# Cache pages shared 9 to 7 between SyncE and GpSimd, and the first gate blocks read ten chunks at a time

## The reference

```
g = jax.nn.softmax(cv, axis=-1)
act = jax.nn.gelu(jnp.einsum('nhkd,nd->nhk', expert_u[experts], x))
y = jnp.einsum('nhk,nhkd->nd', (g * act), expert_v[experts])
```

## Time and profile before

| what | value |
|---|---|
| time, median of three runs | 2148.72 us |
| the profiled execution: own time | 2147.01 us |
| the profiled execution: span | 2145.1 us |
| TensorE busy | 1915.8 us, 89% |
| VectorE busy | 1436.1 us, 67% |
| mean granted TensorE clock | 0.904 |
| granted clock, 400 to 600 us and 600 to 800 us | 0.68 and 0.67 |
| granted clock, 1400 to 1600 us | 1.00 |

### The profile page before, as it was taken

How to read it: one execution, slowest core, us unless ns; L and a number is a source line. 1 busy time by engine, 2 the same in 40 slices (tenths; PEclk the granted TensorE clock), 3 DMA queues, 4 the chain that set the end, 5 groups by cost and what they waited for, 6 DMA issues and landing times.

```text
span 2145.1 us, 26500 instructions
## 1 busy us (share of the span) xinstructions
PE 1915.8 (89%) x9117; PEld 1500.0 (70%) x9117; DVE 1436.1 (67%) x3189; ACT 609.1 (28%) x1020; POOL 586.6 (27%) x454
## 2 busy tenths in 40 slices
PE   6988899666688988999886999999999999999994
PEld 3556674554467745667675788888888888888883
DVE  4025366243346755999986778888888777777777
ACT  1132122210011111114455333333333333333331
POOL 0000002344423123310000114454454444444440
PEclk9989999666675679999998999999999999999997
DMA  6611334354534456554438878999998888888872
GB/s 250 228 40 40 123 118 162 108 164 146 186 137 147 148 171 229 202 178 149 164 141 302 295 278 321 356 349 340 364 340 301 317 289 291 320 287 292 318 255 92
DMA packets 152645, 479.29 MB, mean 223 GB/s; under 512 B 14624, under 2 KB 75856, under 8 KB 130928
## 3 DMA queue, kind: packets, MB, share of 16 engines
q1 hardware_dynamic: 94704, 270.60, 34.8%
q0 software_dynamic: 57856, 207.65, 27.2%
HBM read 443.73 MB, written 33.94 MB: 223 GB/s over the span
## 4 chain that ended last, share of the span: by engine, by line
PE 73%; DVE 16%; another core or an unknown queue 4%; DMA 3%; issue 2%; ACT 2%; POOL 0%; SPq 0%; DVEq 0%; ACTq 0%
PE ps L1034 24%; PE ps L1024 19%; PE ps L634 6%; PE ps L970 3%; PE ps L935 3%; PE ps L986 3%; DVE lo L1650 2%; PE ps L1011 2%; PE ps L721 2%; PE ps L720 2%; PE ps L803 2%; PE ps L743 1%; PE ps L638 1%; DMA lo<-x 1%
## 5 line engine op out<-in xcount | busy, mean ns | idle before, releaser
L1478 POOL DMA_INDIRECT lo<-ur,lo x192 | 244.3, 1272 | 797.8 <-DVE lo L2011 323.5
L1478 POOL DMA_INDIRECT lo<-vr,lo x192 | 278.1, 1448 | 650.1 <-DVE lo L2079 306.7
L1024 PE MATMUL ps<-xh,uh 128*128 128x352 f32 x832 | 270.6, 325 | 0.0
L1024 PE MATMUL ps<-xh,ul 128*128 128x352 f32 x832 | 270.5, 325 | 0.0
L1024 PE MATMUL ps<-xl,uh 128*128 128x352 f32 x832 | 268.8, 323 | 0.0
L1129 ACT ACTIVATE hi<-ps 128x512 f32<-128x512 f32 (+10 forms) x259 | 154.3, 645 | 373.7 <-PE ps L970 111.9
L1034 PE MATMUL ps<-vh,hh 128*128 128x512 f32 (+1 forms) x768 | 240.9, 395 | 19.9 <-DVE vl L2047 19.9
L1034 PE MATMUL ps<-vl,hh 128*128 128x512 f32 (+1 forms) x768 | 241.1, 395 | 0.0
L1034 PE MATMUL ps<-vh,hl 128*128 128x512 f32 (+1 forms) x768 | 240.0, 394 | 0.0
L2071 DVE SCALAR_TENSOR_TENSOR lo<-lo 128x1024 f32<-128x1024 f32 x174 | 221.8, 1282 | 18.5 <-DMA lo<-vr,lo 9.7
L2047 DVE TENSOR_TENSOR vl<-hi,vh 128x1024 fp32r<-128x1024 f32 x128 | 156.9, 1226 | 48.8 <-ACT vh L1129 48.3
(11 more groups left out here) (385 smaller groups left out, 2928.5 us busy)
## 6 DMA issues: line engine op xcount, KB each, us to landing
hi<-ev SPq DMA_DIRECT2D x64, 1024.0 KB
hi<-wts SPq DMA_DIRECT2D x22, 2048.0 KB, 7.8
hi<-eu SPq DMA_DIRECT2D x38, 1024.0 KB, 10.0
lo<-eu SPq DMA_DIRECT2D x26, 1024.0 KB
gates<-hi SPq DMA_DIRECT2D x11, 2048.0 KB, 7.2
hi<-gates SPq DMA_DIRECT2D x32, 704.0 KB, 8.5
lo<-cache SPq DMA_DIRECT2D x48, 128.0 KB
hi<-cache SPq DMA_DIRECT2D x48, 128.0 KB
```

The lines of the kernel that those rows point to most:

```text
L1024: last = nc.tensor.matmul(ps[:, 6 + p, 0:GW[1]], a[p][:, k * 128:(k + 1) * 128], b[:, k, :], start=(k == 0 and b is xh and a is uh), stop= ...
L1478: nc.gpsimd.indirect_dma_start(ring[n % RING], None, table, bass.IndirectOffsetOnAxis(idxs[:, i, k:k + 1], 0)).then_inc(r_in[n % RING], 16)
```

## The change

There are two parts. `SP_PAGES` goes from 12 to 9, so SyncE loads nine of the 16 pages of a round and GpSimd gathers seven. And the first two quads of gates are read from DRAM in two steps: once ten chunks are stored, SyncE reads these ten for both quads (`load_first_gates`), before it stores the last chunk; VectorE copies the last chunk's part from `stage[0]` into `gt`. ScalarE's first `round_v` stands ahead of the copies of the last chunk, its first `round_hidden` ahead of the wait for the last store, and VectorE's first `low_v` ahead of everything of the first block.

```diff
-SP_PAGES = 12
+SP_PAGES = 9
@@ sync
+            def load_first_gates(quad):
+                sp.dma_start(gt[quad].rearrange("p c b t -> p c (b t)")[:, 0:NCH - 1, :],
+                             table[:, 0:NCH - 1, quad * 4:quad * 4 + 4, :].rearrange("e c b t -> e c (b t)")).then_inc(g_in[quad], 16)
...
+                if c == NCH - 1:
+                    sp.wait_ge(gs_in[0], 16 * (NCH // 2))
+                    sp.wait_ge(gs_in[1], 16 * (NCH // 2))
+                    for quad in range(2):
+                        load_first_gates(quad)
                 sp.wait_ge(s["ev_done"], CH // 4 * (c + 1))
                 sp.dma_start(gates[c * NK:(c + 1) * NK, :], stage[c % 2].rearrange("p e t -> p (e t)")).then_inc(gs_in[c % 2], 16)
             load_v(1, 1)
             sp.wait_ge(gs_in[0], 16 * ((NCH + 1) // 2))
-            sp.wait_ge(gs_in[1], 16 * (NCH // 2))
-            for q in range(2):
-                load_gates(q, q)
@@ scalar
                     for q in range((T[i] - S0) // 4, (T[i] - S0 + r) // 4):
+                        if q == (NCH - 1) * CH // 4:
+                            round_v((0, 0), 16, None)
                         gates_copy(q)
...
+            round_hidden(0, 1, None)
             act.wait_ge(gs_in[0], 16 * ((NCH + 1) // 2))
-            round_v((0, 0), 16, None)
-            round_hidden(0, 1, None)
@@ vector
             dve.wait_ge(s["gm_ps"], GW[1] // 4)
+            low_v((0, 0), 1)
+            fetched_gates(0)
+            dve.wait_ge(gs_in[1], 16 * (NCH // 2))
+            dve.wait_ge(s["ev_done"], GW[1] // 4)
+            for quad in range(2):
+                ins = v.tensor_copy(gt[quad][:, NCH - 1], stage[(NCH - 1) % 2][:, quad * 4:quad * 4 + 4, :])
+            step(ins)
             early_gated(0)
             low_hidden(0, 1)
-            low_v((0, 0), 1)
-            fetched_gates(0)
```

## The result

| | before | changed kernel |
|---|---|---|
| median of four runs | 2143.88 us (2138.95 to 2148.87) | 2165.95 us (2158.09 to 2173.91) |
| ratio | | 1.0103, 95% interval 1.0053 to 1.0153 |
| the profiled execution: own time, span | 2147.01, 2145.1 us | 2164.88, 2163.1 us |

The changed kernel is 1.0% slower: the first case, and the sum of the prediction (2164.2 us for the profiled execution) met. That is only half of the story. On the four chips where the experiments ran, the kernel before takes 2079 us instead of 2144, and there the change costs 0.2%, hardly more than nothing. Both halves follow. The chip that it ran on is not on record, so the runs do not say whether it was a fifth chip or one of the four at another time.

What follows compares the result with a forecast made beforehand. TensorE bounds the second half, so sample rounds and the first expert block's start count: 2147.0 + 26.2 (gathers) - 9.0 (gates) = 2164.2 us for the profiled execution, median 2166 us (+0.8%), range 2115 to 2175.

Steps and rivals of the forecast that it cites:

- the first case: Sample rounds: release of VectorE's maximum tied to the end of GpSimd's run; 2157 to 2175 us, chance 0.58.
- Three more gathers in each run: Sample rounds: GpSimd's run ends 3.75 us later, and VectorE's release with it; +26.2 us over rounds 0 to 6.
- the upper end: Sample rounds: distance behind the run's end grows by another 0.5 us for each of 7 rounds; +30 us.
- the pattern: Sample rounds 1 to 6: VectorE's maximum starts 2.2 to 2.7 us behind GpSimd's last gather.
- the reading beneath: Sample rounds: after SyncE's and GpSimd's DMAs issue side by side, engines' signals arrive late until GpSimd's unbroken run ends.
- Gates ten chunks at a time: First expert block: gate reads issued after chunk 9's store let TensorE start earlier; gain 9 us, 7 to 11.
- the release follows SyncE's loads: Sample rounds: three loads less bring the release 2.2 us earlier in 7 rounds, -15.5 us; 2124 us, chance 0.16.
- pages are free: Sample rounds: release not tied to GpSimd's run, only the gates count; 2140 us (2134 to 2143), chance 0.14.
- The late release that goes away: Sample rounds: nine loads stay under the point where signals are held back, saving 57 us; 2083 us, chance 0.12.
- SyncE's tenth load: Sample rounds: condition of the 2083 us rival, that the holding of signals begins only with this load; chance 0.12.
- eight loads: First row fetches: VectorE was already held by "remote" with this many loads issued, argued against the 2083 us rival.

Runs made afterwards that it cites:

- the first comparison: Kernel before against the changed kernel, the measurement of the result table: 2143.88 and 2165.95 us, ratio 1.0103.
- before_again: Kernel before, without any edit, profiled again on one of the chips of the experiments: 2075.62 us in one run.
- g12_quad: Against the kernel before: pages twelve and four, new gate reading with only the first quad's read ahead of the last store; 2065.94 us, ratio 0.9941.
- p9_only: Kernel before with only SP_PAGES changed from 12 to 9, gates read as before: 2087.26 us, ratio 1.0041.

## Why the prediction was right, and where it was not

*Three more gathers in each run: right in the first comparison.* The forecast was 22.5 us for rounds 1 to 6; from the maximum of round 0 (404.72, now 410.97) to that of round 6 (586.15, now 615.03) it was 181.4 and is 204.1 us: 22.6. Two deviations cancel in it: the distance behind the run grew from 2.2 to 2.8 us (the upper end had 0.5 for it), and round 6 was released 3.5 us sooner than the pattern. Round 0, taken at 3.75 us, was held 4.2 us (406.75 to 410.97). Here the reading beneath was luck: the 1.94 us that it stood behind GpSimd's run before was no late release. In `before_again`, without any late signal, the same row stands 1.93 us behind the run, as TensorE's matmul only ends then. That matmul itself ended 2.1 us later in the changed kernel's execution, which nobody forecast. So the rounds end 28.9 us later, not 26.2, and the 26.9 at the gates come close to the forecast only because other stages took 2 us less. The "remote" total is 105.2 us without round 0, forecast 104.

*Gates ten chunks at a time: right.* The steps, in us:

| step | forecast | measured |
|---|---|---|
| issue of the reads to the first product | 5.2 at most | 4.6 |
| first product to TensorE | 1.7 | 1.9 |
| block 0 to block 1 | 7.9 | 8.1 |
| the last store, from its issue | 9.5 | 8.8 |
| block 1 to block 4 | 14.2 | 14.9 |
| gain in all | 9 | 9.1 |

TensorE's first gap shrank further than forecast, to 4.7 us from 7, as the idle time is counted from the end of its last gate matmul, which moved too. The step priced by no row of the trace before, a store behind reads in the queue, was bounded by 0 and 2.7 and taken at 2.2. From 7.3 us before, the store's landing became 8.8 here, 1.5 more. In the four traces of the experiments with both reads ahead it was 9.4 to 10.6, up to 3.4 more, so the upper bound was too low. `g12_quad` shows that the delay is real.

*The rivals.* That the release follows SyncE's loads is refuted by the changed kernel's own trace: 15.1 us from their end to the release with nine loads, 9.8 with twelve. That pages are free is refuted with late signals and without: the rounds of `p9_only` are 7.5 us longer. The late release that goes away (2083 us, chance 0.12, tied to "SyncE's tenth load") did not happen by the change. In the experiments it is absent from the kernel before as well: 2079 us before, 2084 changed. The price of the late releases was near (57 forecast, 59.0 in the rounds) and the condition wrong; that the rival's 2083 us fits the changed kernel's 2083.87 is luck, as it had nothing for GpSimd's full queue. The "eight loads" that the prediction sets against this rival are what its window shows of a burst of twelve; when VectorE started at 336.21 us, not even eight had been issued, so the argument stands.

*What was wrong is the reading beneath.* "Once SyncE's and GpSimd's DMAs have been issued side by side, signals of engines are delivered late": in the experiments they are issued side by side, up to 24 and 13 to a round, and no signal is late in any of twelve traces. The overlap may be needed, but it is not enough. That the last signal is delivered 2.2 to 2.8 us behind the end of GpSimd's run is seen in thirteen rounds of the two first traces (the last of them by ScalarE's wait), before and after the run was lengthened. The change itself was the only edit that moved it, as the late signals never came back. What brings them about, a chip, a state of it or something else, is open.

So 2166 us was met because the trace came from where the result was measured, and the last digits are luck. The fourth run of the kernel before moved its median from 2148.72 to 2143.88 us, so that the medians differ by 22.1 us where 17.2 were forecast; the two profiled executions differ by 17.9. There the parts are +26.9 and -9.1; in the experiments the same two are about +8.5 and -10.6 of a median near 2079 (from the two kernels apart, each within 5 us), and together measured at +3.5 us (0 to 7). The sign of the gates' part is the same in both; the size of the pages' part is not.

## What to carry to other kernels

When a wait has no releaser in the trace, ask first whether the same kernel shows it on another chip or on another day; a schedule tuned against such waits may gain nothing elsewhere. Before a difference of one stage between two traces is explained, see how much that stage varies among traces that do not differ there (here 143 to 158 us). Count the items of the queue that feeds everything (GpSimd's 1.25 us per indirect DMA, here 13 to 19 a round) against the length of a round: below it most of a further item's time was hidden here (7.5 of 26 us showed), above it little (21.6 of 26). And where a transfer on the path stands behind others in a queue, send ahead only what is needed first.

## What the runs showed of the hardware

- The same program with the same instructions took 2145 us of span in one trace and 2074 in another, 58 us of it in six signals of TensorE that arrived 9.2 to 10.3 us late. The median of four runs was 2144 us; in 66 runs on four chips it was 2078 to 2079. Whether the chip or a state of it makes the difference is not known.
- The late signals arrived 2.2 to 2.8 us behind the end of GpSimd's unbroken run of indirect DMAs, in thirteen rounds, whether the run was lengthened or not; one arrived 0.8 us ahead of it.
- GpSimd issued an indirect DMA every 1.25 us, and some took 2 us. With 13 of them in a round of 20.4 us the rounds did not wait for its queue, with 16 the eight rounds together were 7.5 us longer, and with 19 they were 29.1 us longer.
- Without late signals, twenty-four loads of 64 KB issued by SyncE took 12.2 to 14.4 us in the eight rounds, and twelve of 128 KB 6.0 to 6.8 us: 0.5 to 0.6 us for each, whatever its size. In the first comparison, with twelve, it was 6.7 to 8.9 us.
- A 2 MB store landed 7.2 to 7.3 us after its issue with no read ahead of it in SyncE's queue, 7.5 us behind one of 0.66 MB, and 8.8 to 10.6 us behind two.
